# Expert loop in turns of two blocks instead of four

## The reference

```
order = jnp.argsort(flat_e, stable=True)           # 2048 * 8 = 16384 pairs (token, expert), by expert
counts = jnp.bincount(flat_e, length=N_EXPERTS)
padded = (counts + MOE_BLOCK - 1) // MOE_BLOCK * MOE_BLOCK    # MOE_BLOCK = 128
...
def body(acc, blk):                                # one block: 128 rows of one expert
    toks, bw, e = blk
    xb = hp[toks]
    yb = (jax.nn.silu(xb @ w_gate[e]) * (xb @ w_up[e])) @ w_down[e]
    return acc.at[toks].add(yb.astype(f32) * bw[:, None]), None
```

## Time and profile before

| | us |
|---|---|
| median of 3 runs | 2682.56 |
| the profiled execution | 2683.43 |
| its span, first to last instruction | 2681.4 |
| PE busy | 2514.5 (94%) |
| VectorE busy | 1531.1 (57%) |
| ScalarE busy | 1135.7 (42%) |
| POOL busy | 721.4 (27%) |

### The profile page before, as it was taken

The page is one execution under the profiler, slowest core; times in us unless marked ns, Lnnn a source line. Parts: engine busy times, 40 slices in busy tenths (PEclk is TensorE's granted clock), DMA queues, the critical chain, the costliest instruction groups (busy, mean ns, idle before and its releaser), DMA issues. The chain is left out here.

```text
span 2681.4 us, 47699 instructions
## 1 busy us (share of the span) xinstructions
PE 2514.5 (94%) x11413; PEld 1907.9 (71%) x11415; DVE 1531.1 (57%) x2468; ACT 1135.7 (42%) x1743; POOL 721.4 (27%) x830
## 2 busy tenths in 40 slices
PE   6999999968996997999999999999999999999990
PEld 3455555537885786888888888888888888888880
DVE  1454555546777776555566555565555555655535
ACT  2535353433222113544455454554555445554425
POOL 0000000000111001443344333354333333443435
PEclk8999999978998998999999999999999999999995
DMA  6010100027444545887889878898888787987656
GB/s 188 9 55 8 55 8 24 8 58 247 160 149 144 196 165 191 242 257 216 248 252 276 238 224 237 231 269 262 254 255 256 215 242 225 287 256 225 153 115 270
DMA packets 255198, 494.18 MB, mean 184 GB/s; under 512 B 26352, under 2 KB 168592, under 8 KB 255136
## 3 DMA queue, kind: packets, MB, share of 16 engines
q1 hardware_dynamic: 204336, 311.12, 34.2%
q0 software_dynamic: 47952, 179.70, 26.8%
q10 hardware_dynamic: 2848, 2.59, 0.3%
HBM read 363.82 MB, written 129.53 MB: 184 GB/s over the span
## 5 line engine op out<-in xcount | busy, mean ns | idle before, releaser
L1893 POOL DMA_INDIRECT acc<-y,si x164 | 298.4, 1819 | 772.7 <-DMA acc<-y,si 359.5
L1982 DVE TENSOR_TENSOR gu_lo<-raw_gu,gu_hi (+1 forms) x128 | 292.9, 2289 | 173.9 <-ACT gu_hi L1913 173.5
L2090 PE MATMUL psG<-gu_hi,xT_lo 128*128 x1320 | 348.6, 407 | 0.3
L2079 PE MATMUL psG<-gu_hi,xT_hi 128*128 x1328 | 338.7, 398 | 3.1 <-ACT xT_hi L1909 1.6
L2079 PE MATMUL psG<-gu_lo,xT_hi 128*128 x1328 | 337.3, 397 | 0.0
L2079 PEld LDWEIGHTS psG<-gu_hi,xT_hi 128*128 128x128 f32 x1328 | 251.3, 189 | 63.3 <-issue 3.7
L2079 PEld LDWEIGHTS psG<-gu_lo,xT_hi 128*128 128x128 f32 x1328 | 251.2, 189 | 59.9
L2090 PEld LDWEIGHTS psG<-gu_hi,xT_lo 128*128 128x128 f32 x1320 | 237.0, 189 | 45.2 <-issue 1.3
L1913 ACT ACTIVATE gu_hi<-raw_gu (+1 forms) x128 | 238.0, 1908 | 45.7 <-issue 45.7
L645 PE MATMUL psP<-xT,win 128*128 128x512 f32 x512 | 232.5, 603 | 7.2 <-ACT xT L322 4.3
L1982 DVE TENSOR_TENSOR d_lo<-raw_d,d_hi (+1 forms) x64 | 146.7, 2292 | 151.4 <-ACT d_hi L1913 151.4
(11 more groups left out here) (300 smaller groups left out, 3630.9 us busy)
## 6 DMA issues: line engine op xcount, KB each, us to landing
raw_gu<-in_w_gate_dram SPq DMA_DIRECT2D x64, 1024.0 KB, 6.0
raw_gu<-in_w_up_dram SPq DMA_DIRECT2D x64, 1024.0 KB, 12.3
raw_d<-in_w_down_dram SPq DMA_DIRECT2D x64, 1024.0 KB
acc<-out SPq DMA_DIRECT2D x17, 512.0 KB, 3.0
xs<-in_x_dram SPq DMA_DIRECT2D x16, 512.0 KB, 5.3
mT<-mixed SPq DMA_DIRECT2D x16, 512.0 KB, 3.6
xt<-in_x_dram SPq DMA_DIRECT2D x16, 512.0 KB, 4.6
htab<-h SPq DMA_DIRECT2D x16, 512.0 KB, 2.6
```

What stands on the lines that cost most here:

```text
L1893: nc.gpsimd.indirect_dma_start(out=acc, out_offset=bass.IndirectOffsetOnAxis(ap=si[k][:, 0:1], axis=0), in_=y[k][:], in_offset=None, compu ...
L1982: nc.vector.tensor_tensor(dst, src, hi, ALU.subtract).then_inc(dlo_s if n == 2 else gulo_s, 1)
L2079: nc.tensor.matmul(psG[slot][:], xT_hi[slot][:, c, :], right[:, bass.ds(w, 1), c, :].rearrange("p a n -> p (a n)"), start=(n == 0 and c == ...
L2090: m = nc.tensor.matmul(psG[slot][:], xT_lo[slot][:, c, :], gu_hi[:, bass.ds(w, 1), c, :].rearrange("p a n -> p (a n)"), start=False, stop= ...
```

## The change

One constant: the loop body is written for two blocks and the loop has 192 / 2 = 96 iterations instead of 48. With it `n_turns` becomes (blocks + 1) >> 1 instead of (blocks + 3) >> 2. PE reads four words of the table at the start of a body instead of six, ScalarE and VectorE three instead of five. What a block does and in which order is the same.

```diff
@@ -37,7 +37,7 @@
 LRU_C = 8.0
 W_SLOTS = 2
 AHEAD = 4
-TURN = 4
+TURN = 2
 WORDS = BLOCKS + AHEAD
 NEXT_BIT, RANK_BIT, FIRST_BIT = 6, 12, 19
```

## The result

The changed kernel takes 2666.49 us (median of 4 runs, 2664.43 to 2670.31); the kernel before, measured beside it, 2683.42 us (4 runs). The ratio is 0.994, with a 95% interval of 0.9923 to 0.9957: faster by 12 to 21 us. The profiled execution has a span of 2662.6 us against 2681.4.

The account below looks back on a forecast made before the run. PE's own work was taken to bound the loop, with the final norm following the hole. -18.97 (blocks) + 2.3 (boundaries) + 4.1 (skips) = -12.6 us, from 2682.56 to 2670.0 us; range 2664.5 to 2675.

Parts of the forecast that it names:

- Blocks: Expert loop on PE: 161 real blocks round to 162 instead of 164; two fewer at 9.486 us, -18.97 us.
- nothing saved: Rival: near ties in the router make the count 163 or 164 on the chip; 2688 us, chance 0.01.
- Boundaries: Between turns of the loop: 40 more boundaries cost PE nothing to +2.3 us; +2.3 taken.
- The prediction's own rival: The rival "lead not rebuilt": all 2.3 us of disturbance from four late boundaries, 0.57 us each; chance 0.04.
- The lower bound, nothing: Low end for PE's cost of added boundaries: zero, since the block interval over a boundary showed none.
- the lead is rebuilt within two blocks: PE's sequencer, 0.7 us ahead of the array at a boundary, is 3.7 us ahead again two blocks later.
- lead not rebuilt: Rival: PE's sequencer has 0.7 us left at a boundary, and lateness stalls the array; +44, 2712 us, chance 0.04.
- the other rival: VectorE reaches HT_lo late in blocks with splits: +8 to +15 us, 2676 to 2683 us, chance 0.06.
- Skips: Hole behind the loop: 15 skipped iterations instead of 7 delay POOL's drain, +4.1 us.
- Both bounds: Skips' cost: +2.4 us (PE's line) if POOL's drain counts from the scatter, +4.1 if from its own start.
- The sum: Whole kernel: -18.97 + 2.3 + 4.1 = -12.6 us, median to 2670.0 us.
- The rule against it: Each turn's branch back forces an instruction fetch and stall; as a rival, 40 exposed fetches give 2708 us, chance 0.01.

Follow-up runs that it names:

- the kernel that takes floor and remainder: Changed kernel with floor(blocks/2) turns as the loop's end and one single block behind it if the count is odd, no skips: 2652.59 us, ratio 0.9872 to before.
- the second table read: Changed kernel with PE's table read made twice at each boundary: 2702.84 us in one run.

## Why the prediction was right, and where it wasn't

**Blocks.** -18.97 us was forecast, and the loop has two intervals of 9.487 less. The run with 164 blocks in turns of two takes the gain away and with it the whole change: 1558.06 us of loop. The count of 161, worked out from the reference, stands: 162 scatters ran, and the kernel that takes floor and remainder ran 161. Of the rivals, "nothing saved" is out.

**Boundaries.** The forecast of 2670.0 us is 3.5 above the measured 2666.49, and most of that is this term. It was mis-sized: +2.3 us forecast, while the profiles show -1.7 and +0.3 for the change and 0.0 with 164 blocks. To put the disturbance on the boundaries was right, since each long interval crosses one. The step that failed is the next one: I divided 2.3 us evenly over 41 boundaries, 0.057 each, and carried that on to 40 more. It is a few single late boundaries, two to seven of 0.1 to 1.1 us in the kernels with turns of two, four of 0.4 before; the sum varies from 0.5 to 2.9 us between profiles of these kernels and doesn't follow the number of turns (2.18 us with 41, 2.20 with 82). The prediction's own rival had described four late boundaries of 0.57 us each; its sum did not use that. The lower bound, nothing, was the right end, and the interval of 9.49 over a boundary had said so. That the lead is rebuilt within two blocks held: PE is busy for 380.00 of 380 us. The rival "lead not rebuilt" named the right mechanism, and it exists: with the second table read it costs 0.9 us at 40 boundaries. What was missing was its size. The prediction had PE's table read shrink with its words; it went from 0.82 us to 0.33 at every second boundary and to 1.00 at the others. At these the distance ahead of L2090 is 0.54 us, not the 0.7 that I took for all, and 0.2 of it are usable, so this change is closer to that edge than the forecast knew. The gap of the other rival, VectorE late at HT_lo, did not open at two and four blocks a turn; at eight it did.

**Skips.** +4.1 forecast, +3.8 measured. POOL's eight skips cost 5.2 us and took the place of 1.15 us of waiting, as worked out; the drain took 5.46 us instead of 5.79, which is the 0.3 between them. Both bounds had been kept because it was open whether the drain counts from its own start. It does: with 162 blocks it starts 6.0, 10.2 or 18.6 us behind the last scatter in different kernels, and its length stays at 5.46.

**The sum.** -12.6 forecast; the mechanisms measured give -18.97, +3.8 and 0 for the boundaries, so -15.2; the medians give -16.9 and -17.8, with intervals of 12 to 21 and 15 to 22 us. What remains between -15.2 and the medians is 2 to 3 us, no more than the start of the loop varies by (1049.4 to 1057.9 us) in kernels that are alike up to there. Where it comes from stays open.

**The rule against it.** The forecast put it at 0.01 because 41 turns had shown no fetch. That was right for this change: the changed loop has no packet of an instruction queue from 1090 to 2585 us either. Ahead of it, from 1030 to 1090 us, the kernel before has six packets of q14 beside the three of q8 that the prediction counted. But the reason given, that a branch back finds its code, holds only up to a length. With eight blocks, 124 fetches and 126 us appear, and both go with VectorE's loop. The Trainium skill, Runtime: NRT & Kernel Launch, section Instruction fetch mechanics, says that a taken branch whose target has left the window of two pages forces a fetch; the run with eight agrees with it (5.5 us behind the branch). The prediction's "by that rule 41 turns would have fetched" left out the condition: the rule speaks only of targets that have left the window, so four blocks without a fetch don't speak against it. That they lie inside the window is a reading, not shown: no run moved the length in smaller steps, and length in instructions alone doesn't decide between engines. In a turn of eight VectorE's sequencer passes through 316 instructions at most and fetches; with VectorE's loop cut to two, PE's passes through 715, matmuls not counted, and there are two packets in the whole loop.

## What to carry to other kernels

Where an engine is full in a loop, padding of the trip count costs whole iterations: count them from the data and look how far the rounding goes, then price what a shorter turn adds outside the loop, above all iterations that are counted but skipped, since those stand where nothing hides them. A loop end in a register did away with them for nothing here. Before unrolling further, look at the instruction queues' packets inside the loop; none at four blocks became 124 at eight, and the loop was disturbed for 126 us, a part of it because the clock fell behind the stops. Not all of that need be the fetches, as a longer body also reads more of the table at once.

## What the runs showed of the hardware

POOL's drain at the end of a stage in which it issued indirect DMAs takes microseconds, and its length goes with the number of blocks; where in the hole it began and how long the turns of two or four were made no difference: 5.30 us with 161 blocks, 5.46 with 162 (five kernels), 5.79 with 164 (three), which is 0.16 us for each block of two DMAs, and yet 1.95 with 168 (two kernels, both with turns of eight on POOL). Why it is shorter there stays open.

A read of four table words by PE took 0.33 or 1.00 us, alternately from one boundary to the next. The words read begin alternately at a multiple of four words (the last turn, 0.33) and two words off it (the turn before, 1.00), so the place is the likely cause, which wasn't tested by itself. Six words, always from a multiple of four in the kernel before, took 0.82.

A skipped iteration, a branch, an addition, another branch, a move and an increment, costs 0.89 us on PE's sequencer and 0.65 on POOL's, and 0.90 and 0.65 with fifteen of them. The sixteen added behind these, whose inner branch compares the other way round, cost 0.90 on PE and 0.53 on POOL.
